# A decoder trunk on one core: VectorE's order of work in the first body of the second mixer's first in-projection

## The reference

```
c_act = silu(c)
for i in (0, 1):
    mod = c_act @ ada_w[i] + ada_b[i]          # 2048 x 12288 per layer
    sh1, sc1, g1, sh2, sc2, g2 = split(mod, 6)
    h = x * (1 + sc1) + sh1
    y = mixer_i(h)                             # h @ w_in, heads and channels, @ w_out
    x = layer_norm(ALPHA * x + (1 + g1) * y)
    h = x * (1 + sc2) + sh2
    y = (silu(h @ w_gate) * (h @ w_up)) @ w_down
    x = layer_norm(ALPHA * x + (1 + g2) * y)
```

## Time and profile before

| | us |
|---|---|
| median of 3 runs | 2792.78 |
| lowest, highest | 2791.82, 2797.11 |
| the profiled execution, its own time | 2795.02 |
| its span | 2793.4 |
| TensorE (PE) busy | 2560.1 |
| VectorE (DVE) busy | 2052.8 |
| ScalarE (ACT) busy | 1215.5 |

### The profile page before, as it was taken

How to read it: one execution, slowest core, us unless ns; L and a number is a source line. 1 busy time by engine, 2 the same in 40 slices (tenths; PEclk the granted TensorE clock), 3 DMA queues, 4 the chain that set the end, 5 groups by cost and what they waited for, 6 DMA issues and landing times.

```text
span 2793.4 us, 41999 instructions
## 1 busy us (share of the span) xinstructions
PE 2560.1 (92%) x16532; PEld 2314.8 (83%) x16532; DVE 2052.8 (73%) x2526; ACT 1215.5 (44%) x1606; POOL 198.8 (7%) x226
## 2 busy tenths in 40 slices
PE   1299999888789999999999899998999999999998
PEld 1298887777788899889988899998978898899887
DVE  7779999878487777777778888568787655555556
ACT  0145556544445443444343453453454434443444
POOL 0012222100000000000001011000000000000000
PEclk6599999888899999999999999999999999999998
DMA  8864444455447888888888589545668655555552
GB/s 354 298 226 136 153 155 156 164 184 168 139 164 271 272 284 276 285 275 283 277 281 274 172 314 346 176 159 201 222 229 283 226 196 194 185 193 195 185 193 76
DMA packets 272987, 616.02 MB, mean 221 GB/s; under 512 B 23211, under 2 KB 23746, under 8 KB 272578
## 3 DMA queue, kind: packets, MB, share of 16 engines
q1 hardware_dynamic: 240194, 488.04, 51.4%
q0 software_dynamic: 32640, 125.84, 13.0%
HBM read 611.73 MB, written 2.10 MB: 220 GB/s over the span
## 4 chain that ended last, share of the span: by engine, by line
PE 79%; DVE 13%; ACT 2%; issue 2%; DMA 2%; SPq 1%; DVEq 0%; POOL 0%; POOLq 0%
PE groups L2507 12%; PE groups L2511 11%; PE groups L2509 11%; PE groups L2499 11%; PE groups L2501 11%; PE groups L2503 11%; PE pc L2678 1%; DMA ada_units<-in_ada_w_dram 1%; DVE ada_acc L2356 1%; PE pb L2668 1%; SPq L1647 1%; DVE ada_acc L2005 1%; DVE w_lo L2023 1%; DVE ada_acc L860 1%; PE pm L2474 1%
## 5 line engine op out<-in xcount | busy, mean ns | idle before, releaser
L1726 ACT ACTIVATE w_hi<-w_raw 128x1024 fp32r<-128x1024 f32 x776 | 817.1, 1058 | 1207.5 <-PE groups L2503 545.3
L2023 DVE TENSOR_TENSOR w_lo<-w_raw,w_hi 128x1024 fp32r<-128x1024 f32 x749 | 908.8, 1223 | 554.2 <-ACT w_hi L1726 550.2
L2499 PE MATMUL groups<-w_hi,act_hi 128*128 128x512 f32 x1408 | 554.0, 393 | 20.1 <-DVE act_lo L2156 20.1
L2507 PE MATMUL groups<-act_hi,w_hi 128*128 128x256 f32 x1776 | 518.6, 292 | 46.2 <-DVE act_lo L2277 17.8
L2503 PE MATMUL groups<-w_lo,act_hi 128*128 128x512 f32 x1408 | 550.3, 391 | 0.0
L2501 PE MATMUL groups<-w_hi,act_lo 128*128 128x512 f32 x1408 | 550.2, 391 | 0.0
L2509 PE MATMUL groups<-act_lo,w_hi 128*128 128x256 f32 x1776 | 510.8, 288 | 0.0
L2511 PE MATMUL groups<-act_hi,w_lo 128*128 128x256 f32 x1776 | 510.2, 287 | 0.0
L2507 PEld LDWEIGHTS groups<-act_hi,w_hi 128*128 128x128 f32 x1776 | 349.4, 197 | 58.7 <-issue 51.5
L2507 PE MATMUL groups<-hid_hi,w_hi 128*128 128x256 f32 x1392 | 388.4, 279 | 0.0
L2511 PE MATMUL groups<-hid_hi,w_lo 128*128 128x256 f32 x1392 | 387.0, 278 | 0.0
(11 more groups left out here) (436 smaller groups left out, 2495.1 us busy)
## 6 DMA issues: line engine op xcount, KB each, us to landing
ada_units<-in_ada_w_dram POOLq DMA_DIRECT2D x120, 1024.0 KB, 6.6
w_raw<-in_ffn_w_gate_dram SPq DMA_DIRECT2D x88, 1024.0 KB, 5.3
w_raw<-in_ffn_w_up_dram SPq DMA_DIRECT2D x88, 1024.0 KB, 5.3
w_raw<-in_ffn_w_down_dram SPq DMA_DIRECT2D x88, 1024.0 KB, 5.1
w_raw<-in_cd_w_in_dram SPq DMA_DIRECT2D x48, 1024.0 KB, 6.2
w_raw<-in_ab_w_in_dram SPq DMA_DIRECT2D x40, 1024.0 KB, 5.9
ada_units<-in_ada_w_dram SPq DMA_DIRECT2D x80, 512.0 KB, 4.5
ada_first<-in_ada_w_dram SPq DMA_DIRECT2D x24, 1024.0 KB, 10.2
```

What stands on the lines that cost most here:

```text
L1726: act.activation(whi[:, half, k], raw[:, slot, k], ACT.Copy).then_inc(hi_done, 1)
L2023: dve.tensor_tensor(wlo[:, half, k], raw[:, slot, k], whi[:, half, k].bitcast(F32), ALU.subtract).then_inc(lo_done, 1)
L2499: pe.matmul(dst, hi[:, k, rows], whi[:, j % 2, kk], start=(k == 0), stop=False, skip_group_check=True)
L2507: pe.matmul(dst, whi[:, j % 2, kk, cols], hi[:, k], start=(q == 0 and kk == 0 and n % 2 == 0), stop=False, skip_group_check=True)
```

## The change

In the first body of in1a (positions j = 0 to 7 with i = 0), two things change. VectorE's order within a position becomes norm piece, split, ada units. The counts of ada units become [0, 1, 1, 2, 1, 1, 2, 0]: none in position 0, two in position 3, eight in all as before. The two looped bodies keep order and counts, and so do all other products. TensorE's, ScalarE's, GpSimd's and SyncE's programs are untouched.

```
-BEHIND_NORM = ("up00", "up10")
-ADA_BEHIND_NORM = {(1, 8): [0, 0, 0, 1, 1, 1, 1, 0]}
+BEHIND_NORM = ("up00", "in1a", "up10")
+ADA_BEHIND_NORM = {(1, 8): [0, 0, 0, 1, 1, 1, 1, 0], (2, 8): [0, 1, 1, 2, 1, 1, 2, 0]}
...
                         if before and behind_norm:
                             before(i, j)
-                        for _ in range((ADA_BEHIND_NORM if behind_norm else ADA_AT)[p["ada"], p["bu"]][j]):
-                            ada_unit(p["ab0"] + taken // 4 + p["ada"] * i, taken % 4, taken // 4, ada_in_pool,
-                                     2 * ADA_FIRST + (0 if p["name"] == "in0u" else DN_BLOCKS))
-                            taken += 1
+                        def ada_units(taken):
+                            for _ in range((ADA_BEHIND_NORM if behind_norm else ADA_AT)[p["ada"], p["bu"]][j]):
+                                ada_unit(p["ab0"] + taken // 4 + p["ada"] * i, taken % 4, taken // 4, ada_in_pool,
+                                         2 * ADA_FIRST + (0 if p["name"] == "in0u" else DN_BLOCKS))
+                                taken += 1
+                            return taken
+                        behind_split = p["name"] == "in1a" and behind_norm
+                        if not behind_split:
+                            taken = ada_units(taken)
                         u = p["u0"] + p["bu"] * i + j
                         if before and not behind_norm:
                             before(i, j)
                         if not (p["bodies"] == 1 and u + 2 >= n_units) and not (skip_last and j == p["bu"] - 1):
                             split_lo((j + 2 - lag) % 4, (j - lag) % 2, u + 2 - lag,
                                      1 if hold and j == p["bu"] - 1 else HALVES)
+                        if behind_split:
+                            taken = ada_units(taken)
```

## The result

Over 11 runs of each, the changed kernel's median is 2802.62 us and that of the kernel before 2793.83 us; the ratio is 1.0032, with a 95% interval from 1.0020 to 1.0043. The change made the kernel slower by 0.3%, or 8.8 us, against a forecast of +4.5 us (+0.16%). The median lies 1.1 us above the upper end of the stated range, 2801.5.

The account below looks back on a forecast made before the run. TensorE, busy 92% of the span, was taken as the bound, so VectorE's order pays only where TensorE waits for it. +3.5 + 1.7 - 0.7 = +4.5 us on 2792.8 gave 2797.3 us, range 2791.5 to 2801.5.

Parts of the forecast that it names:

- positions 4 to 7: First body of in1a: ada units queued behind splits that need TensorE's progress put the second ada_sum +3.5 us late.
- A5 and A7: Sixth and eighth ada units of in1a's first body, forecast to end at 1640.7 or 1643.5 and at 1653.2 us.
- the late A0: First ada unit of in1a's first body, forecast to end at 1612.55 instead of 1600.76, 11.8 us later.
- the bounds for A3: Position 3, fourth ada unit: reached between 1624.9 and 1626.6 as unit 3 frees the split's slots, ended 1628.5 to 1629.6.
- The price of a load: Ada load for the first body's eighth ada unit: taken to land 5.9 us after issue, at 1650.0.
- The clock: TensorE at half speed behind the first body's last three stalls, 1.7 us each, and none behind the first.
- The term of 1.7 us behind the second sum: Half speed of TensorE after the first body's second ada_sum, adding 1.7 us to the +3.5.
- Later bodies: End of in1a's third body: the old 0.78 us wait for VectorE's last ada unit goes, -0.7 us; the rest merely starts later.
- the term of -0.7 us: End of in1a's third body: the vanished 0.78 us wait for VectorE's last ada unit, counted as a gain.
- The crowded rival: First body of in1a: loads of 8.0 us and all the clock losses, +5.6 to +9.0 us; chance 0.29.

Follow-up runs that it names:

- g4: Changed kernel with in1a's ada loads cut to a quarter and the ada units ahead of the split again in positions 4 to 7; ratio 0.9992 to the kernel before.
- f1: Changed kernel with ada units behind the norm piece but ahead of the split, and in1a's ada loads cut to a quarter; ratio 0.9995 to the kernel before.
- f2: Changed kernel with in1a's ada loads cut to a quarter (128 of 512 rows), order and counts kept; ratio 1.0025 to the kernel before.
- e3: Changed kernel with the ada units behind the norm piece but ahead of the split, new counts and whole loads; ratio 1.0009 to the kernel before.
- g1: Kernel before with TensorE's wait for ScalarE's copy of in1a's last group moved behind in1b's first unit; ratio 0.9992 to the kernel before.
- f4: Changed kernel with TensorE's wait for ScalarE's copy of in1a's last group moved behind in1b's first unit; ratio 1.0014 to the kernel before.
- e2: Kernel before with only the new ada counts, in the old order (ada units, norm piece, split); ratio 1.0006 to the kernel before.
- g3: The changed kernel itself, unaltered, measured and traced a second time; ratio 1.0025 to the kernel before.
- g2: Kernel before with ada counts [1, 0, 1, 2, 1, 1, 2, 0] in the old order and the attention's copy wait moved; ratio 0.9991 to the kernel before.
- e1: Kernel before with only the new order (norm piece, split, ada units) in the first body, old counts; ratio 1.0024 to the kernel before.

## Why the prediction came out as it did

**The mechanism in the first body was right for the most part.** The forecast had unit 2 at 14.7 us behind unit 0, unit 3 at 23.3, the first sum at 39.2 and the second at 62.8. The trace has 14.8, 23.4, 39.3 and 62.5, with waits of 2.9 and 3.2 us where 2.7 and 3.6 were forecast. The gain of 6.1 us at unit 3 came and was given back at the two sums. g4 shows the reason named under positions 4 to 7, A5 and A7 behind splits which wait for TensorE. Of the first wait the forecast said that everything hangs on the late A0. f1 against f2 shows otherwise: with A0 late in both, the wait comes only with the ada units behind the splits, and the changed kernel's trace has A2 and A3 behind unit 5's split and its 0.47 and 1.59 us of waiting. The forecast priced this place only as part of the bounds for A3. The stall ahead of unit 2 was 0.47 us and not 1.8, because TensorE was at half speed up to +5.9 in this execution and up to +2.9 in the one of before, ahead of everything that was changed; the start of unit 2 is set by act_lo and did not move.

**The price of a load.** I took 5.9 us for A7's; it was 5.5. f2 shows that this hardly mattered in this order, 0.3 us between loads of 5.5 and 3.0. Loads of 8.0 us, for which the forecast had the second sum at 1655.4 to 1657.4, did not come ahead of it. That VectorE's lateness spaced the loads out is my inference; e3 shows a 9.6 us load in the order that does crowd them. The Trainium skill, page "DMA: Bandwidth & Descriptors", section "Anatomy of one DMA — SWDGE (gpsimd) path", gives by its fit 2.6 us for the quarter loads, an estimate, and they took 2.7 to 4.2 with a median of 2.9, close to it. For 1 MB the estimate by it is 4.4 us, under every such load of in1a, the shortest of which took 5.5; the measurement decides.

**The clock.** Half speed of 3.4 us behind the second, third and fourth of the new stalls and none behind the first is what came. The premise, that stalls from 2.63 us on are followed by it, does not hold in general (last section), so this hit is in part luck. The term of 1.7 us behind the second sum measured 1.6: the third sum is 4.9 us late, the second 3.3.

**The step that failed** is "Later bodies", the term of -0.7 us, and what I wrote of the rest of the kernel, that it "starts later by the sum, in the same state". The wait of 0.78 us at the last sum did go, and the last sum is 4.0 us late and not 4.9. But behind it TensorE waits for ScalarE's copy of in1a's last group, in the function that hands over to in1b. In the kernel before the 0.78 us covered this; in the changed one it became a wait of 1.05 us, so in1b's first unit is again 4.9 us late. The refund was none. It had also been read from a single trace: g1's, with the same in1a as the kernel before, has no such wait. And then a half-speed stretch followed which the kernel before did not have: the first attention matmul is 6.4 us late, 1.5 more. f4 shows what the wait costs in the changed kernel: with it moved, both wait and stretch went and the hand-over took 2.6 us less. But the stretch is not shown to be the change's own: e3's trace has it behind the same 0.78 us as the kernel before, and e2's lacks it behind the same 1.05 us as the changed one. Up to in1b's first unit the loss is 4.9 us; the other 1.5 may fall on either kernel from one execution to the next. In these two traces, the term was -0.7 and measured +1.5: 3.5 + 1.7 - 0.7 = 4.5 should have been 3.3 + 1.6 + 0 + 1.5 = 6.4.

**What this leaves.** The measured median is 5.3 us above the forecast of 2797.3. Of these, 1.0 come from the base, whose median rose from 2792.8 to 2793.8 with more runs, 1.9 from the terms above, and 2.4 have no cause shown. 6.4 us is 0.23% of the time, inside both intervals, but under the 8.8 us between the medians of the first comparison. The traces give 6.4 and, for g3, 6.7 us up to the attention. f4's trace of the same first bodies shows one way to lose more, 2.9 us at later sums, in one of three executions. Whether this fills the rest was not settled: the part behind the attention alone took between 1034.8 and 1041.9 us over these traces. The crowded rival, which had the right size, had the wrong reason. Its sum was also added up wrongly: a second sum at 1657.4 gives 7.7 + 1.7 - 0.7 = +8.7 and not +7.8, so its upper end should have been +9.9, or 2802.7 in place of 2801.8.

## What to carry to other kernels

When a wait is shortened by moving other work behind it, follow the moved work to its own consumer: here it had a fixed place in TensorE's in-order queue, and moving this place only showed the next instruction of VectorE that was late. A small wait which disappears is a gain only if nothing else was running beneath it; look for what the waiting engine meets next before counting it back. And where two streams of loads run at once, see when each load can be issued: e3 waited 5.73 us at the second sum with whole loads and not at all with small ones.

## What the runs showed of the hardware

In the same bodies the half-speed stretches repeat: 3.4 us each behind stalls of 2.54 to 2.56, of 2.89 or 2.90 and of 3.22 to 3.54 us in all three traces (changed, f4, g3), and none behind 0.47 to 0.49. But over all traces the length of the stall does not decide. The granted clock stayed at 1.00 behind 2.55 us at unit 3 in e3, behind 3.25 and 3.23 us at unit 2 in e2 and g2, and behind 2.72 us ahead of the attention in g1 and g2, while 0.62 us ahead of a sum in f4 was followed by 3.4 us at 0.50. In e1 and e3, around the stalls of 4.67 and 5.73 us, it was at 0.50 for 6.8 us.

At the hand-over to in1b, ten traces have a wait of TensorE, for the sum, for the copy or for both, of 0.78 to 1.05 us in all; half speed followed in eight and not in those of the kernel before and of e2. In the three where the wait was moved and the last sum had none (f4, g1, g2), none followed.

The time from issue to landing of the same 1 MB load ranged from 5.5 to 9.9 us within this product (9.9 in f4's second body), and in the first body up to the 9.6 us of e3, in which TensorE then waited 5.73 us; yet e3's ratio, 1.0009, is lower than its trace alone would suggest. So a single trace shows which waits there are, and not what they cost on average.
